# Score matmuls of two neighbouring heads alternate between the two halves of the array

## The reference

```python
proj = x @ w_in                      # q, k, v of 8 sliding-window heads (2 kv heads) and of 8 MoBA heads, width 64
# sliding window, 128 keys incl. self, with a sink:
logits = q k^T * 64**-0.5 - slope[h] * dist          # masked outside the window
m = max(max(logits), sink);  p = exp(logits - m)
o = (p / (sum(p) + exp(sink - m))) @ v
# MoBA, blocks of 256 keys, top 3: with 512 tokens every past block is chosen, so this is causal attention
o = softmax(q k^T * 64**-0.5 - slope[h] * dist) @ v
return concat(o_window, o_moba) @ w_out
```

## Time and profile before

| | |
|---|---|
| median of 3 runs | 2031.14 us (2031.06 to 2031.51) |
| profiled execution, its own time | 2030.7 us |
| its span in the profile | 2029.0 us |
| granted TensorE clock, mean | 0.994 |
| busy: PE, DVE, ACT, POOL | 98%, 53%, 31%, 44% |

### The profile page before, as it was taken

The page is one execution under the profiler, slowest core; times in us unless marked ns, Lnnn a source line. Parts: engine busy times, 40 slices in busy tenths (PEclk is TensorE's granted clock), DMA queues, the critical chain, the costliest instruction groups (busy, mean ns, idle before and its releaser), DMA issues.

```text
span 2029.0 us, 25118 instructions
## 1 busy us (share of the span) xinstructions
PE 1986.2 (98%) x10329; PEld 1691.4 (83%) x10329; DVE 1082.9 (53%) x1495; ACT 630.3 (31%) x782; POOL 901.0 (44%) x598
## 2 busy tenths in 40 slices
PE   8999999999999999999999999999999999999997
PEld 7888888988878888888988888898988988888886
DVE  2556572554255566573555656363544663477545
ACT  3333332343332333322333332232222223233320
POOL 4554364622214535464455546443433344454533
PEclk9999999999999999999999999999999999999999
DMA  6232323321104231322423132231221104323221
GB/s 230 90 112 89 105 84 104 103 69 42 63 22 145 83 104 63 125 96 91 146 82 105 63 125 92 95 119 48 69 78 63 47 24 138 125 84 109 92 90 42
DMA packets 135138, 185.46 MB, mean 91 GB/s; under 512 B 3168, under 2 KB 119024, under 8 KB 135024
## 3 DMA queue, kind: packets, MB, share of 16 engines
q1 hardware_dynamic: 134864, 183.59, 27.2%
q10 hardware_dynamic: 160, 0.26, 0.1%
HBM read 181.48 MB, written 2.10 MB: 90 GB/s over the span
## 4 chain that ended last, share of the span: by engine, by line
PE 92%; DVE 4%; POOL 3%; ACT 1%; issue 0%; DMA 0%; SPq 0%; DVEq 0%; ACTq 0%
PE psum L1373 28%; PE psum L1374 28%; PE psum L1375 27%; PE psum L1633 3%; POOL w_lo L663 2%; PE psum L1578 2%; PE psum L1609 1%; PE psum L1394 1%; PE psum L1593 1%; DVE x L1047 0%; ACT w_hi L725 0%; DVE x L1207 0%; PE psum L1661 0%; PE psum L1671 0%; DMA raw<-in_ffn_w 0%
## 5 line engine op out<-in xcount | busy, mean ns | idle before, releaser
L663 POOL TENSOR_TENSOR w_lo<-raw,w_hi 128x512 fp32r<-128x512 f32 x524 | 846.2, 1648 | 964.0 <-ACT w_hi L725 939.5
L1373 PE MATMUL psum<-xt_hi,w_hi 128*128 128x512 f32 (+1 forms) x1824 | 679.4, 372 | 11.9 <-DVE xt_lo L946 7.5
L1374 PE MATMUL psum<-xt_lo,w_hi 128*128 128x512 f32 (+1 forms) x1824 | 674.3, 370 | 0.0
L1375 PE MATMUL psum<-xt_hi,w_lo 128*128 128x512 f32 (+1 forms) x1824 | 674.0, 369 | 0.0
L1373 PEld LDWEIGHTS psum<-xt_hi,w_hi 128*128 128x128 f32 x1824 | 347.2, 190 | 76.4 <-issue 11.2
L1375 PEld LDWEIGHTS psum<-xt_hi,w_lo 128*128 128x128 f32 x1824 | 347.0, 190 | 57.5
L1374 PEld LDWEIGHTS psum<-xt_lo,w_hi 128*128 128x128 f32 x1824 | 347.3, 190 | 55.7
L725 ACT ACTIVATE w_hi<-raw 128x2048 fp32r<-128x2048 f32 x133 | 253.6, 1910 | 308.5 <-PE psum L1375 307.8
L1007 DVE SCALAR_TENSOR_TENSOR x<-psum,x 128x512 f32<-128x512 f32 x224 | 145.4, 683 | 129.4 <-PE psum L1375 125.6
L739 ACT ACTIVATE gate<-psum 128x512 f32<-128x512 f32 x88 | 52.5, 598 | 309.8 <-PE psum L1375 309.8
L1047 DVE SCALAR_TENSOR_TENSOR x<-psum,x 128x512 f32<-128x512 f32 x128 | 86.2, 687 | 111.3 <-PE psum L1375 111.0
(11 more groups left out here) (151 smaller groups left out, 2252.3 us busy)
## 6 DMA issues: line engine op xcount, KB each, us to landing
raw<-in_ffn_w SPq DMA_DIRECT2D x116, 1024.0 KB, 5.4
raw_odd<-in_ffn_w SPq DMA_DIRECT2D x16, 1024.0 KB, 5.1
raw<-in_hgrn_w_in SPq DMA_DIRECT2D x16, 1024.0 KB, 5.4
raw<-in_attn_w_in SPq DMA_DIRECT2D x9, 1024.0 KB, 5.4
raw<-in_attn_w_out SPq DMA_DIRECT2D x4, 1024.0 KB, 5.0
raw<-in_hgrn_w_out SPq DMA_DIRECT2D x4, 1024.0 KB, 4.8
lng<-in_ln_g SPq DMA_DIRECT2D x6, 512.0 KB, 4.2
lnb<-in_ln_b SPq DMA_DIRECT2D x6, 512.0 KB, 5.3
```

Source lines behind the costliest of these rows:

```text
L663: op = pool.tensor_tensor(w_lo[:, slot_of[s], cols], raw[:, slot_of[s], cols], w_hi[:, slot_of[s], cols].bitcast(F32), ALU.subtract)
L1373: pe.matmul(out_, w[0], xs[0], start=first, stop=False)
L1374: pe.matmul(out_, w[0], xs[1], start=False, stop=False)
L1375: return pe.matmul(out_, w[1], xs[0], start=False, stop=last)
```

## The change

Units are formed of two neighbouring heads and fewer tiles. A window pair has two units (tiles 0 and 1; tiles 2 and 3), a MoBA pair three (tiles 0 and 1; tile 2; tile 3). There are 20 units in place of 24. In a unit the score matmuls go tile by tile, first the even head on rows 0-63 into bank 2, then the odd head on rows 64-127 into bank 3. VectorE adds distances once for each head, from bank 2 and from bank 3, and takes the maxima of both heads in one or two reductions; the minimum with the sinks is one operation for both heads. `probs` and `probs_t` become two buffers of 1024 columns each. The transposes of a unit fill bank 4 and part or all of bank 5, so that VectorE always copies a part. A pair is kept at once, with one multiplication for each head. The quarters are dealt out anew in `FILLS` (0, 1 or 2 after turn_probs and values of each unit).

```diff
-UNITS = [0, 4, 8, 16, 24]
-TURN_OUT_AT = {5: 0, 12: 1, 19: 2}
-WITHOUT_FILL = (17, 20, 22)
+UNITS = [0, 4, 8, 14, 20]
+TURN_OUT_AT = {5: 0, 10: 1, 16: 2}
+FILLS = {u: (int(u != 18), 0 if u < 2 else 2 if 8 <= u < 12 else 1 if u < 15 else 0) for u in range(UNITS[4])}
...
-            steps += fill(u not in WITHOUT_FILL)
+            steps += fill(FILLS[u][0])
             if u in TURN_OUT_AT:
                 steps.append(("turn_out", TURN_OUT_AT[u]))
 
-            steps += [("values", u)] + fill(2 <= u <= UNITS[3])
+            steps += [("values", u)] + fill(FILLS[u][1])
...
-SWA_UNIT = ([(0, [0]), (1, [0, 1]), (2, [1, 2]), (3, [2, 3])], P)
-MOBA_UNITS = [([(0, [0]), (2, [0, 1, 2]), (1, [0, 1])], 0), ([(3, [0, 1, 2, 3])], 0)]
+SWA_UNITS = [[(0, [0]), (1, [0, 1])], [(2, [1, 2]), (3, [2, 3])]]
+MOBA_UNITS = [[(0, [0]), (1, [0, 1])], [(2, [0, 1, 2])], [(3, [0, 1, 2, 3])]]
...
-        probs = cut(3, 7 * P)
-        probs_t = cut(2, 7 * P)
+        probs = cut(2, 8 * P)
+        probs_t = cut(2, 8 * P)
...
             def exponentials(u):
...
+                for i in range(2):
+                    head = 2 * pair + i
+                    for n_, (tile, keys) in enumerate(tiles):
+                        part = probs[:, u % 2, at:at + len(keys) * P]
+                        k = i * len(tiles) + n_
+                        op = act.activation(part, part, ACT.Exp, bias=neg_max[:, u % 3, k:k + 1],
+                                            accum_out=sums[:, head % 4, tile:tile + 1])
+                        at += len(keys) * P
+                    if head < 8:
+                        op = act.activation(sink_part[:, head % 4, tiles[0][0]:tiles[0][0] + 2],
+                                            neg_max[:, u % 3, 2 * i:2 * i + 2], ACT.Exp, bias=sink_b[:, head:head + 1])
                 op.then_inc(exp_done, 1)
...
             def logits(u):
...
-                if u >= 3:
-                    dve.wait_ge(probs_turned, u - 2)
...
+                if u >= 2:
+                    dve.wait_ge(probs_turned, u - 1)
+                for i in range(2):
+                    op = dve.scalar_tensor_tensor(out=probs[:, u % 2, i * width:(i + 1) * width], in0=table,
+                                                  scalar=-SLOPES[2 * pair + i],
+                                                  in1=psum[:, (2 + i) * T:(2 + i) * T + width],
+                                                  op0=ALU.mult, op1=ALU.add)
+                op.then_inc(scores_kept, 1)
...
             def scores(u, blocks_needed):
...
-                at = 2 * T + col
+                at = 0
                 for tile, keys in tiles:
...
+                    for i in range(2):
+                        rows = slice(i * HD, (i + 1) * HD)
+                        kt = k_swa[rows, g, :] if pair < 4 else k_moba[rows, g % 2, pair % 2, :]
+                        mm = pe.matmul(psum[:, (2 + i) * T + at:(2 + i) * T + at + len(keys) * P],
+                                       q_t[rows, g % 2, pair % 2, tile * P:(tile + 1) * P],
+                                       kt[:, keys[0] * P:(keys[-1] + 1) * P], start=True, stop=True)
                     at += len(keys) * P
                 mm.then_inc(scores_done, 1)
...
+                for i in range(2):
+                    cols = slice((of_group + i) * HD, (of_group + i + 1) * HD)
+                    op = dve.tensor_tensor(att_out[pair // 2 % 2][:, :, cols],
+                                           bank[6 + i][:, 0:NT * HD].rearrange("p (t n) -> p t n", n=HD),
+                                           inv_sum[:, i, :, None].broadcast_to([P, NT, HD]), ALU.mult)
+                op.then_inc(head_kept, 1)
```

More of the change, by code:

```diff
@@ L315, in build_trunk @@
         sink_part = sb("sink_part", [P, 4, 4])
-        inv_sum = sb("inv_sum", [P, 4])
-        total = sb("total", [P, 4])
+        inv_sum = sb("inv_sum", [P, 2, 4])
+        total = sb("total", [P, 2, 4])
         sink_b = sb("sink_b", [P, 8])
@@ L642, in attention_tables @@
             def attention_tables():
-                for table, (tiles, _) in [(dist_swa, SWA_UNIT), (dist_moba[0], MOBA_UNITS[0]), (dist_moba[1], MOBA_UNITS[1])]:
+                for table, tiles in [(dist_swa, SWA_UNITS[0] + SWA_UNITS[1])] + list(zip(dist_moba, MOBA_UNITS)):
                     at = 0
@@ L823, in exponentials @@
             def exponentials(u):
-                head, tiles, _, _ = attention_unit(u)
+                pair, tiles, _, _ = attention_unit(u)
                 act.wait_ge(neg_max_ready, u + 1)
                 at = 0
[L827 to L834, removed]
+                for i in range(2):
[9 more added lines that the diff above has]
+                                            neg_max[:, u % 3, 2 * i:2 * i + 2], ACT.Exp, bias=sink_b[:, head:head + 1])
                 op.then_inc(exp_done, 1)
@@ L1058, in logits @@
             def logits(u):
-                head, tiles, col, _ = attention_unit(u)
-                width = sum(len(keys) for _, keys in tiles) * P
-                table = dist_swa if u < 8 else dist_moba[u % 2]
+                pair, tiles, k, _ = attention_unit(u)
+                width = unit_blocks(u) * P
+                table = (dist_swa[:, 3 * P * k:3 * P * k + width] if u < UNITS[2] else dist_moba[k])
                 dve.wait_ge(scores_done, u + 1)
-                if u >= 3:
-                    dve.wait_ge(probs_turned, u - 2)
@@ L1066, in logits @@
[L1066 to L1069, removed]
-                dve.wait_ge(scores_kept, u + 1)
[L1071 to L1075, removed]
@@ new lines, in logits @@
+                op.then_inc(scores_kept, 1)
+                dve.wait_ge(scores_kept, u + 1)
+                both = probs[:, u % 2, 0:2 * width]
+                if len(tiles) == 1 or len(tiles[0][1]) == len(tiles[1][1]):
+                    n_ = 2 * len(tiles)
+                    op = dve.tensor_reduce(neg_max[:, u % 3, 0:n_], both.rearrange("p (a n) -> p a n", a=n_), AX.X,
+                                           ALU.max, negate=True)
+                else:
+                    split = len(tiles[0][1]) * P
+                    heads = both.rearrange("p (h n) -> p h n", h=2)
+                    per_tile = neg_max[:, u % 3, :].rearrange("p (h n) -> p h n", h=2)
+                    dve.tensor_reduce(per_tile[:, :, 0], heads[:, :, 0:split], AX.X, ALU.max, negate=True)
+                    op = dve.tensor_reduce(per_tile[:, :, 1], heads[:, :, split:], AX.X, ALU.max, negate=True)
@@ L1078, in logits @@
+                if u < UNITS[2]:
                     op.then_inc(max_ready, 1)
                     dve.wait_ge(max_ready, u + 1)
-                    op = dve.tensor_scalar(neg_max[:, u % 3, :], neg_max[:, u % 3, :], neg_sink[:, head:head + 1],
-                                           None, ALU.min)
+                    per_head = neg_max[:, u % 3, :].rearrange("p (h n) -> p h n", h=2)
+                    op = dve.tensor_tensor(per_head, per_head,
+                                           neg_sink[:, 2 * pair:2 * pair + 2][:, :, None].broadcast_to([P, 2, 2]), ALU.min)
@@ L1082, in logits @@
                 op.then_inc(neg_max_ready, 1)
             def probs_second_bank(u):
[L1085 to L1093, removed]
+                dve.wait_ge(probs_turned, u + 1)
@@ L1094, in keep_head, with keep_heads @@
+                dve.tensor_copy(probs_t[:, u % 2, 4 * P:2 * unit_blocks(u) * P],
+                                bank[5][:, 0:(2 * unit_blocks(u) - 4) * P]).then_inc(probs_t_dve, 1)
+            def keep_heads(u):
+                pair, _, _, ends = attention_unit(u)
                 if not ends:
                     return
-                dve.wait_ge(head_done, head + 1)
+                dve.wait_ge(head_done, pair + 1)
                 dve.wait_ge(exp_done, u + 1)
-                sum_ = sums[:, head % 4, :]
@@ L1099, in keep_head @@
-                if head < 8:
-                    then(dve.tensor_tensor(total[:], sum_, sink_part[:, head % 4, :], ALU.add))
+                of_group = 2 * (pair % 2)
+                sum_ = sums[:, of_group:of_group + 2, :]
+                if pair < 4:
+                    then(dve.tensor_tensor(total[:], sum_, sink_part[:, of_group:of_group + 2, :], ALU.add))
                     sum_ = total[:]
                 then(dve.reciprocal(inv_sum[:], sum_))
-                dve.tensor_tensor(att_out[head // 4 % 2][:, :, (head % 4) * HD:(head % 4 + 1) * HD],
-                                  bank[6 + head % 2][:, 0:NT * HD].rearrange("p (t n) -> p t n", n=HD),
-                                  inv_sum[:, :, None].broadcast_to([P, NT, HD]), ALU.mult).then_inc(head_kept, 1)
+                for i in range(2):
[3 more added lines that the diff above has]
+                                           inv_sum[:, i, :, None].broadcast_to([P, NT, HD]), ALU.mult)
@@ L1565, in scores @@
             def scores(u, blocks_needed):
-                head, tiles, col, _ = attention_unit(u)
-                g = head // 4
```

(29 more changed lines are left out.)

20 lines of the change are left out of this document (10 added, 10 removed).

## The result

The changed kernel takes 2015.99 us (median of 4 runs, 2013.98 to 2016.76) against 2031.1 us before, a ratio of 0.9927 with a 95% interval of 0.9914 to 0.9940: 15.1 us or 0.7% faster. The direction was forecast; the size was not.

What follows compares the result with a forecast made beforehand. The prediction took TensorE's instruction stream to bound the kernel. Its terms, -8.2 - 1.6 + 0.2 = -9.6 us, gave 2021.5 us from the median of 2031.14; the likeliest case's range was 2019.0 to 2023.5, the whole range up to 2030.3.

Steps and rivals of the forecast that it cites:

- Alternation (a): Attention score matmuls: alternating heads on two array halves lets their records overlap, saving 7.4 to 9.1 us, taken as 8.2.
- The records start in order: Score matmuls: records start in issue order, each waiting until its own half is done with the one before.
- 2n records take n + 1 slots: Score units: A's second record shares a slot with B's first, so eight 256-column records take five slots, saving 0.65 us.
- the load limit: Units with tiles 0 and 1: eight weight loads in line, up to 0.108 us each, cut the saving from 0.43 to 0.22.
- Fewer units (b): Attention stage: 24 units become 20, each saving 0.40 us of entry to and exit from 64-row matmuls, 1.6 us in all.
- waits (d): TensorE idle at four places: unit 4's scores +0.4, third turn_out -0.6, last turn_out +0.4, unit 18 unchanged; together +0.2 us.
- VectorE and ScalarE (c): Attention logits and copies: VectorE's logits per sliding-window pair stay 5.2 us; nothing on the path except where the waits say so.
- No overlap: Rival on score matmuls: the array takes one fp32 record at a time, whichever half; 2029.7 us, chance 0.17.
- A cost at each change of half: Rival on score matmuls: 44 inner changes of half cost 0.2 us each, with no overlap; 2038.5 us, chance 0.09.
- overlap, but paid for: Rival on score matmuls: full overlap, but 0.1 us paid at each change of half; 2025.9 us, chance 0.06.
- VectorE or ScalarE: Rival in the attention stage: one of these engines becomes the new bound; could add a microsecond, no chance given.

Runs made afterwards that it cites:

- e1_same_half: The changed kernel with both heads of a pair reading q and k on partitions 0-63, so all score matmuls use rows 0-63; 2028.86 us.
- e5_four_times: The changed kernel with all even-head score matmuls of a unit issued before the odd head's, each head's issued four times into the same place; 2098.28 us.
- e2_head_by_head: The changed kernel with all tiles of the even head issued before those of the odd head in each unit, nothing left out; 2015.1 us.

## Why the prediction was wrong

**Alternation (a): the halves do overlap, but more closely than predicted.** Predicted -8.2 (7.4 to 9.1), measured -14.4 by putting both heads on one half, 14.8 a copy by repetition. The failed step is "The records start in order", from which "2n records take n + 1 slots" followed. I had let B's first record wait for the start of A's second. It starts with A's first (two records at 405.78): 2n records take n slots. The second failed step is the load limit: I took 0.108 us for a weight load out of full-height work and put eight of them in one line, but the loads of the two halves start together (two at 405.78). It took about 0.9 us off the middle of the range. With n slots the term is half of the serial streams, 4 x (1.30 + 1.74) + 4 x (1.30 + 1.30 + 1.74) = 29.5, so 14.8. The range was made only from the in-order picture with and without the load limit, and the full factor of two was not among its bounds, although two half-height streams that share nothing would have given it. That omission put the result outside the range.

**Fewer units (b) and waits (d).** Predicted -1.6 + 0.2 = -1.4, measured -1.9 in the trace of `e1_same_half`. No run changes the number of units alone; with the waits at -0.17, as below, 1.75 us are left for four crossings, 0.44 each, near the 0.40 of the prediction. The 0.11 that a first record adds is not the price of the crossing alone: in `e5_four_times` B's first record has the longer slot too (first record 480 ns, at 412.76), in the middle of 64-row work. Of the waits, unit 4's scores stand idle 0.55 us where 0.8 was predicted (0.26 printed before). ScalarE's chain did end later, and the copy of q ended at 423.31, as the second row shows:

```profile
420.35 1.89 PE L1627 MATMUL psum<-arena 128*128 128x64 f32 x16
...
422.74 0.57 ACT L795 ACTIVATE arena<-psum 128x512 f32<-128x512 f32 x1
...
423.45 0.89 PE L1594 MATMUL psum<-arena 64*128 64x128 f32 x7 [0.55 <-ACT arena L795]
```

The projection behind unit 3's scores starts at 417.49 and the copy at 422.74, so 5.25 us, not 5.4, and scores follow after 5.96, not 6.1. The transposes behind the third turn_out do not wait at all (0.2 predicted, 0.82 before). The last turn_out waits 1.09 (1.1 predicted), the values of unit 18 wait 0.73 (0.73 predicted). These changes sum to +0.29 - 0.82 + 0.36 = -0.17 us.

**VectorE and ScalarE (c)** stayed off the path, as predicted. One reduction of 1024 columns takes 1.22 us as estimated and an addition of 384 columns 0.551 against 0.55:

```profile
L1071 DVE SCALAR_TENSOR_TENSOR arena<-arena,psum 128x384 f32<-128x384 f32 x24 | 12.2, 551 | 21.0 <-PE psum L1594 21.0
...
L1080 DVE TENSOR_REDUCE neg_max<-arena 128x4 f32<-128x1024 f32 x4 | 4.9, 1220 | 0.1
```

**The sum as it should have been**: -14.8 - 1.6 - 0.2 = -16.6 us, against 16.3 in the distance and 15.1 between the medians.

**The rivals.** No overlap is refuted by the pairs of starts. A cost at each change of half is refuted as well: `e2_head_by_head` has one change a unit where the changed kernel has three in the two-tile units, 24 fewer, and the distance differs by 0.10 us, where even the 0.1 a change of "overlap, but paid for" would have given 2.4. VectorE or ScalarE did not become the bound: TensorE still carries 92% of the chain that ended last.

## What to carry to other kernels

Where a matmul uses 64 rows, pair it with one on the other half of the rows and in another PSUM bank: here the fp32 pair took the time of one, and the gain was half of the serial streams to within 3%. Alternate them, or let no more than two matmuls of one half stand in front of the other's; four-fold runs of one head cost 40.0 us more than the same work alternated (distances of 281.32 and 241.34). When costing an overlap that no row shows, put full sharing of the time among the bounds, and when a quarter of work is moved under a wait, look for what it covered before, in the queue of the engine that answers.

## What the runs showed of the hardware

Two fp32 matmuls of 64 rows on different halves and banks start within 0.02 us of each other (first record 405.78, two at once), with their weight loads paired too. A matmul of one half started ahead of an earlier one of the other half (B1 of `e2_head_by_head`, ahead of A2), but in `e5_four_times` never with more than two unfinished ones in front of it. The Trainium skill, "TensorE: Matmul & The Clock Gate", section Part 3: Packing small matmuls, has different row groups run at once, which these runs confirm; it also has matmuls start strictly in program order, and `e2_head_by_head` shows otherwise (B1's records before A2's), so the measurement decides. Changing the half cost nothing measurable (24 changes, 0.10 us), while a crossing into 64-row work and out again costs about 0.40 us, of which 0.11, the first record's longer slot, is seen without a crossing too. The rest is in agreement with "TensorEngine Tiling (Array Packing)", section Key Properties, which has a change of mode drain the array and a change of tile not.
